# Linear attention on one core: where DVE forms the first two levels' products

## The reference, cut to what matters

```python
q, k, v, r, z_f, z_b = split(h @ w_in)                 # 4 heads, key width 128, value width 256
log_g  = -softplus(-(z @ w_g2 + bias)) / GLA_TAU       # per direction, head and key channel
b      = cumsum(log_g, axis=time)                      # within a chunk
scores = einsum("bnihd,bnjhd,bnijhd->bnhij", q, k, exp(b_i - b_j))   # causal, i >= j
o      = scores @ v + (q * exp(b)) @ s_enter           # and the states carried from chunk to chunk
```

## Time and profile before

| what | value |
|---|---|
| median of 3 runs | 1550.83 us (1549.01 to 1551.13) |
| the profiled execution | 1551.89 us, its span 1550.2 us |
| PE busy | 1510.7 us, 97% of the span |
| DVE busy | 1120.4 us, 72% |
| ACT busy | 660.5 us, 43% |
| POOL busy | 169.0 us, 11% |
| clock granted to PE, mean | 0.99 of full speed |

### The profile page before, as it was taken

How to read it: one execution, slowest core, us unless ns; L and a number is a source line. 1 busy time by engine, 2 the same in 40 slices (tenths; PEclk the granted TensorE clock), 3 DMA queues, 4 the chain that set the end, 5 groups by cost and what they waited for, 6 DMA issues and landing times.

```text
span 1550.2 us, 25482 instructions
## 1 busy us (share of the span) xinstructions
PE 1510.7 (97%) x9222; PEld 1483.7 (96%) x9222; DVE 1120.4 (72%) x1709; ACT 660.5 (43%) x953; POOL 169.0 (11%) x260
## 2 busy tenths in 40 slices
PE   8999999999979999999999999999889999999998
PEld 7999999989979999999999999998779999999998
DVE  4798888879987877789887767986977575444432
ACT  4533342369955333332343333225555553333321
POOL 0001000000120000001000000100894000000000
PEclk9999999999979999999999999999999999999999
DMA  9666676513432655667455566753222134334421
GB/s 374 220 245 213 231 244 223 193 59 119 141 108 96 218 190 188 203 222 239 162 188 182 193 193 213 250 190 113 69 81 82 55 109 149 122 131 140 151 94 41
DMA packets 68282, 257.09 MB, mean 166 GB/s; under 512 B 7584, under 2 KB 8608, under 8 KB 67968
## 3 DMA queue, kind: packets, MB, share of 16 engines
q1 hardware_dynamic: 48944, 187.57, 35.9%
q0 software_dynamic: 18512, 67.58, 13.0%
q10 hardware_dynamic: 768, 1.19, 0.2%
HBM read 253.68 MB, written 2.63 MB: 165 GB/s over the span
## 4 chain that ended last, share of the span: by engine, by line
PE 86%; DVE 7%; ACT 3%; POOL 2%; issue 1%; DMA 0%; SPq 0%; DVEq 0%; ACTq 0%
PE bank L557 26%; PE bank L559 25%; PE bank L558 25%; DVE tmp_a L1560 2%; DVE h_lo L1579 1%; ACT w_hi_sb L1006 1%; DVE w_lo_sb L1472 1%; PE wide L859 1%; PE bank L570 1%; PE bank L636 1%; PE bank L881 0%; DVE bcum L2046 0%; ACT rgs L1253 0%; DMA x<-in_x 0%; PE bank L898 0%
## 5 line engine op out<-in xcount | busy, mean ns | idle before, releaser
L1006 ACT ACTIVATE w_hi_sb<-raw 128x1024 fp32r<-128x1024 f32 (+3 forms) x308 | 344.1, 1122 | 475.7 <-PE bank L559 451.6
L557 PE MATMUL bank<-h_hi,w_hi_sb 128*128 128x384 f32 x1567 | 529.2, 338 | 3.6 <-DVE tmp_a L1684 1.4
L1472 DVE TENSOR_TENSOR w_lo_sb<-raw,w_hi_sb 128x1024 fp32r<-128x1024 f32 (+3 forms) x308 | 403.3, 1310 | 172.1 <-ACT w_hi_sb L1006 169.3
L559 PE MATMUL bank<-h_hi,w_lo_sb 128*128 128x384 f32 x1567 | 526.6, 336 | 0.0
L558 PE MATMUL bank<-h_lo,w_hi_sb 128*128 128x384 f32 x1567 | 526.6, 336 | 0.0
L557 PEld LDWEIGHTS bank<-h_hi,w_hi_sb 128*128 128x128 f32 x1567 | 294.6, 188 | 8.0 <-DVE w_lo_sb L1472 3.0
L558 PEld LDWEIGHTS bank<-h_lo,w_hi_sb 128*128 128x128 f32 x1567 | 294.7, 188 | 0.0
L559 PEld LDWEIGHTS bank<-h_hi,w_lo_sb 128*128 128x128 f32 x1567 | 294.6, 188 | 0.0
L557 PE MATMUL bank<-a_hi,w_hi_sb 128*128 128x384 f32 x704 | 236.8, 336 | 1.5 <-DVE a_lo L1695 1.5
L559 PE MATMUL bank<-a_hi,w_lo_sb 128*128 128x384 f32 x704 | 236.6, 336 | 0.0
L558 PE MATMUL bank<-a_lo,w_hi_sb 128*128 128x384 f32 x704 | 236.5, 336 | 0.0
(11 more groups left out here) (313 smaller groups left out, 1600.1 us busy)
## 6 DMA issues: line engine op xcount, KB each, us to landing
raw<-in_ffn_in SPq DMA_DIRECT2D x176, 512.0 KB, 3.5
ada_raw<-in_ada_w POOLq DMA_DIRECT2D x128, 512.0 KB, 3.5
raw<-in_ffn_out SPq DMA_DIRECT2D x64, 704.0 KB, 4.3
raw<-in_rg_in SPq DMA_DIRECT2D x20, 512.0 KB, 3.3
ada_first<-in_ada_w SPq DMA_DIRECT2D x8, 1024.0 KB, 17.4
raw<-in_rg_out SPq DMA_DIRECT2D x8, 640.0 KB, 3.9
raw<-in_gla_qk SPq DMA_DIRECT2D x8, 512.0 KB, 3.5
raw<-in_gla_v SPq DMA_DIRECT2D x8, 512.0 KB, 3.2
```

The costliest lines, as they stand in the source:

```text
L557: pe.matmul(out, w_hi_sb[:, slot, w], hi[k], start=start and j == 0, stop=False)
L559: last = pe.matmul(out, w_lo_sb[:, slot, w], hi[k], start=False, stop=stop and j == len(ks) - 1)
L1006: A(w_hi_sb[:, s, 0:w], raw[:, s, 0:w], ACT.Copy).then_inc(w_hi, 1)
L1472: V.tensor_tensor(w_lo_sb[:, s, 0:w], raw[:, s, 0:w], w_hi_sb[:, s, 0:w].bitcast(F32), ALU.subtract).then_inc(w_split, 1)
```

## The change

DVE forms the products of levels 1 and 2 of head 0 at another place. Before, both stand behind the last head's scans and what follows them. After, when the last head's gates are made, the product of level 1 stands ahead of the two subtractions, and the product of level 2 between the subtractions and the scans. The function `level_keys` is defined earlier for this, with the same text. Which instructions run, their operands and their semaphores stay as they are.

```diff
--- before.py
+++ after.py
@@ -2021,6 +2021,14 @@
                 V.tensor_scalar(qk[:, b // 2, b % 2, :], bank[b % RING][:, 0:T], 1.0 if b % 2 else QSCALE, None,
                                 ALU.mult).then_inc(drained, 1)
 
+            def level_keys(n):
+
+                hd, l = divmod(n, NLEV + 1)
+                if l:
+                    k = hd * NLEV + l - 1
+                    dve.wait_ge(e_ready, k + 1)
+                    V.tensor_tensor(e_slot[k % 4], e_slot[k % 4], qk[:, hd, :, :], ALU.mult).then_inc(qkt_ready, 1)
+
             for b in range(RING):
                 take_qk(b)
                 ahead(BASE["gla_qk"] + b)
@@ -2036,10 +2044,14 @@
                         V.tensor_scalar(tmp_b[:, dr, 0:T], bank[4 + (u0 + dr) % 4][:, 0:T], gla_b[:, dr, hd:hd + 1],
                                         0.0, ALU.add, ALU.min).then_inc(zz_drained, 1)
                     made = seq.value()
+                    if hd == HEADS - 1:
+                        level_keys(1)
                     for dr in range(2):
                         dve.wait_ge(zz_drained, u0 + dr + 1)
                         lg = tmp_b[:, dr, 0:T]
                         seq.mark(V.tensor_tensor(lg, lg, zz_tmp[(u0 + dr) % 4], ALU.subtract))
+                    if hd == HEADS - 1:
+                        level_keys(2)
                     for dr in range(2):
                         dve.wait_ge(dve_seq, made + dr + 1)
                         back = slice(None, None, -1) if dr else slice(None)
@@ -2077,14 +2089,6 @@
                                                   bank[2][:, j * DV:(j + 1) * DV], ALU.mult, ALU.add)
                 last.then_inc(st_ready, 1)
 
-            def level_keys(n):
-
-                hd, l = divmod(n, NLEV + 1)
-                if l:
-                    k = hd * NLEV + l - 1
-                    dve.wait_ge(e_ready, k + 1)
-                    V.tensor_tensor(e_slot[k % 4], e_slot[k % 4], qk[:, hd, :, :], ALU.mult).then_inc(qkt_ready, 1)
-
             def take_values(j):
                 dve.wait_ge(w_used, BASE["gla_r"])
                 V.tensor_copy(vt[:, j // 2, 512 * (j % 2):512 * (j % 2) + 512], bank[V_BANKS[j]][:, :]
@@ -2122,8 +2126,6 @@
                                     ALU.subtract).then_inc(og_ready, 1)
 
             V.tensor_scalar(spare[:, 0:DC], gla_g, 0.5, None, ALU.mult).then_inc(half_g, 1)
-            for n in LEVELS_AT[0]:
-                level_keys(n)
             for s in range(2 * DC):
                 here, ahead_of = list(LEVELS_AT[s]), list(LEVELS_AT[s + 1])
                 if s - 1 in TURN_AT:
```

## The result

The changed kernel takes 1553.19 us, median of 13 runs, beside 1549.89 for the kernel before: ratio 1.0018, 95% interval 1.0011 to 1.0025. By the ratio it is slower by 2.8 us (the two medians lie 3.3 apart), where 1.4 us less was forecast, and the time lies above the range, which ended at 1552.2.

The account below looks back on a forecast made before the run. PE, busy 97% of the span, bounds the kernel. Terms 0.0, 0.5 and 1.2 sum to 1.7 us, or 1.2 if the first wait lowers the clock; 1.4 taken off the median 1550.83 gives 1549.4 us, range 1547.0 to 1552.2.

Parts of the forecast that it names:

- what was moved past: Head 3's scans end 1.74 us later, value block 3's split and SP's load 1.7; cost 0, at most 0.1 us.
- the gain on PE from level 1: First term, at level 2: the wait moves there from level 1, level 2 starts no earlier, 0.0 us.
- The drain's delay: Before level 2: GpSimd lengthens DVE's exposed scan, split and product, 0.31 us each; 0.6 us taken, at most 0.93.
- The second term: GpSimd's second level starts 0.5 us earlier, bounds 0.2 and 1.1, so level 12 is released 0.5 us earlier.
- The third term: Behind level 12: the shorter wait leaves PE's clock up, 1.2 us gained, bounds 0 and 1.61.
- The fall behind level 2: Before level 2: a 3.4 us wait may bring the clock down; PE 1.6 us later again, 2.2 in all.
- the slow rival: At level 2: DVE held back 0.93, clock falls, PE 2.5 us late; 0.8 us slower, 1551.6 us; chance 0.14.
- decision point: The slow case decides once PE's 2.5 us exceed the 2.2 GpSimd's slot behind level 5 spared, less GpSimd's own gain.
- my objection to it: Against the slow case: both clock falls are needed, and the second wait would be short after the first.

Follow-up runs that it names:

- e5: The changed kernel again, unchanged, timed and profiled beside the kernel before: ratio 1.0015 (1.0006 to 1.0024).
- e6: On the changed kernel, only the first product stays moved; the second goes back behind the small copies: ratio to the kernel before 1.0013.
- e2: On the changed kernel, GpSimd's level k = 4 is held until DVE's small copies of chunk ends are done: ratio to the kernel before 1.0002.
- e3: On the changed kernel, DVE's drain of level 0 goes right behind the second product, ahead of the scans: ratio to the kernel before 1.0005.
- e4: On the changed kernel, PE does level 2 behind the first third of value block 1, levels 3 and 4 one third later: ratio to before 1.0004.
- e9: On the changed kernel, split of value block 3, small copies and halving of the gain move behind step 0's merges: ratio to before 1.0001.
- e7: The kernel before, unchanged, profiled a second time for its stage; not timed.

## Why the prediction was wrong

**Right.** The 2.76 us before level 1 go. They come back before level 2, ended by the drain of level 0 (2.83 us, and 4.15 in e5, where 3.1 to 3.7 was given: the q/k phase's fall was not reckoned with). The products don't wait for ScalarE, what was moved past (SP's load, the readers of the scans) costs nothing, and the gain on PE from level 1 is 0.

**The drain's delay.** Put at 0.6 us with an upper bound of 0.93, it is 1.16, and 1.33 in e5. In the first profile the counted instructions (scan, split, product) kept their lengths, and the five small ones behind the split took it all. In e5 scans and split together lost 0.71, near what was counted for two, and the small copies 0.63 on top. I had counted the small ones as free. The mechanism was right; the bound left out the instructions that exceed it.

**The second term.** GpSimd was to be 0.5 us ahead at k = 5. It is 0.01 behind (10.56 and 10.55), since the e-slot that it waits for is read by level 2, which the drain delays.

**The third term, where the sign was lost.** The step said: after the change PE comes to level 12 with its wait at 2.2 us or less, so I expect the clock to hold, for a gain of 1.2. The wait is 1.9 us, and the clock fell in four profiles of four and in e6, while with waits of 2.4 to 2.8 it held in two of four of the kernel before, and in e2, e3, e4 and e9. The length of the wait was no guide. What went with it was the fall before: the clock fell behind level 12 in all six profiles with a fall behind level 1 or 2 (e7, e6 and four of after), and in one of seven with a wait there but no such fall (before). That is a count, not a cause. And the 1.2 us could at most be had in executions that fall before the change; two of four don't. Nor was it 1.2: from level 12 to r takes 21.7 us with the fall behind level 12 (57.37 - 35.71) and 20.9 without (56.62 - 35.70), so by r one such fall costs 0.75 us.

The fall behind level 2 was foreseen, at 1.6 us for PE, but its price at level 12 was taken off an advance of GpSimd's that does not exist. It let GpSimd begin k = 8 0.47 us late, the longer instructions of k = 8 added 0.6, and level 12 is 1.1 us late. This is the slow rival's path, place and decision point included, but for the small instructions in place of the counted ones and the 0.6; it had 0.14 and a price of 0.8 us. Its condition was met, and my objection to it (the second wait would be short, so no second fall) was wrong.

**The size.** The stage gives 58.67 - 57.11 = 1.6 us in the mean over four profiles each. The timings say 2.8 and 2.3 us. The mean of the stage mixes executions with and without the fall in the q/k phase. Like with like it is 1.7 us without (59.32 against the mean of 57.37 and 57.83) and 1.8 with (58.45 against 56.62). Of the 1.8, 1.07 is there at level 12 and 0.76 is the second fall. e5's interval (0.9 to 3.7 us) holds this, that of the first timing (1.7 to 3.9) has it at its edge. Behind the stage both kernels take the same 394.6 to 394.7 us. Ahead of it, the mark lies between 1097.15 and 1098.91 in four profiles of before and between 1096.72 and 1099.21 in four of after, which is too wide to tell a microsecond. That the rest of the 2.8 is chance, or more falls in unprofiled executions, is not shown. What also stays open is why the clock fell behind waits of 1.9 us in one kernel and held behind 2.8 in another.

## What to carry to other kernels

When an instruction is moved ahead to end one wait, follow the waiting engine to its next wait and ask whether that one falls due at the same time as before: here the sum of DVE's work up to the next release was unchanged, so the wait only moved on. Ask too which engine the earlier release sets free, and whether its work makes the instructions on the path longer. A long wait can cost PE's clock on top of itself, and not in every execution. Two ways brought the stage back in one profile each: work that PE has anyway, put into the wait (e4, r at 56.70), and work of DVE taken out of the stretch ahead of the release (e9, 56.05).

## What the runs showed that was not expected

- Five DVE instructions of four or eight elements took 1.68 us beside GpSimd, 0.53 alone (0.37 + 0.16 in e2). Being small did not protect them; only in e5 the last of them kept its 0.16.
- A GpSimd instruction of 0.50 us took 1.73 when it met DVE's last scan and the split behind it.
- Each time that PE's clock fell in the profiles read, it stayed down for about 3.4 us, in one case (e5) twice that; one such stretch makes PE 1.6 us late (levels 12 to 13 take 3.74 us with it, levels 1 to 2 take 2.13 without).
- Executions of one and the same kernel differ by up to 1.2 us in this stage alone (56.62 to 57.83), and the difference is that of their falls: 0.45 us from the one behind level 1, 0.75 from the one behind level 12.
